# Per-head sums of squares in two float32r products, one quarter later, and the first values scaled ahead of a half subtraction

## The chip, the cores and the metric

The kernel runs on one core of one Trainium2 chip. The metric is device microseconds of one execution, inputs and output in the chip's memory; lower is better. A kernel's time is the median of its runs.

## The reference

Two transformer blocks on 256 tokens of width 1024, in float32. The change is in the second block's mixer, in the part that goes through heads. Cut to what matters:

```python
q_g = l2norm(cq.reshape(B, S, GDN_QK_HEADS, GDN_DK)) * GDN_DK ** -0.5
k_g = l2norm(ck.reshape(B, S, GDN_QK_HEADS, GDN_DK))
# l2norm(x) = x * rsqrt(sum(x * x over the 128 features of a head) + 1e-6)
kb = k * beta[..., None]
A = where(strict, einsum('bhntk,bhnsk->bhnts', kb, k) * Lmat, 0.0)
T = triangular_solve(eye + A, eye)                 # unit lower triangle, per chunk
u = matmul(T, v * beta[..., None]); w = matmul(T, kb * exp(gam)[..., None])
# per chunk: v_new = u - w S; o = (q exp(gam)) S + (q k^T Lmat) v_new; S = decayed S + k^T v_new
o_g = rmsnorm(o_g, gdn_out_norm) * silu(gz)        # and, beside it, the HGRN branch o_h
```

So for each head the squares of the convolved q and k are summed over the 128 features, which lie on the partitions: a product with a matrix of ones gives every partition the sum of each token's column.

## The kernel before, in words

**Exact products in pieces.** Weights arrive in chunks of 2048 columns x 128 partitions in a ring of three slots. ScalarE rounds a chunk to float32r (`split`, L590, or in halves with `split_part`, L597), VectorE writes the remainder (`low_of`, L1101; a whole chunk in `w_low`, halves in `w_low_half`), and TensorE does three float32r products for each one of the reference (`three`, L1860 to L1862; `three_x`, L1865 to L1867). A few small products inside a head use plain float32, and each of those shows as two MATMUL records.

**The heads.** One loop body `head(i, gemm, main)` runs on each of TensorE, ScalarE and VectorE, for i = 0 with `gemm` alone, for i = 1 to 7 in a hardware loop with both, and for i = 8 with `main` alone. The `gemm` part projects head i (six weight chunks), convolves, normalises and prepares its matrices; the `main` part does the recurrences of head i - 1: a level-by-level solve of the unit triangle (`inv_z`, L2365; `inv_w`, L2381; `inv_t`, L2390, with VectorE's masked merge `inverse`, L1638, and ScalarE's copies), the level-wise HGRN scores (L2342), the two chunks' values and the output. Order on each engine is the order of the written code; engines meet through semaphores only, and an engine that waits for one does nothing else.

**TensorE's order.** The projection is cut in 24 quarters of 12 products, 0 to 15 by column (256 columns each), 16 to 23 by token (512 columns each), and the small products stand between them by hand. Around the change, for i = 1 to 7: quarter 12; the first chunk's values (L2420, `vn0_done`); HGRN values (L2425 to L2427); quarter 13; wait for `vn0_ready`, the cross product L2440 (`cross_done`); quarter 14; wait for `r1_ready`, L2446 (`vn1_done`); wait for `sq_ready`, the sum of squares L2454 into bank 2 of M (`ss_done`); quarter 15; wait for `hsq_ready`, transposes of the gated HGRN output L2434 (`hss_done`); wait for `vn1_ready`, the output of the delta branch L2463 to L2465 (`go_done`); L2471 (`gam_done`); quarters 16 and 17; wait for `rs_ready`, L2480 (`vt_done`); quarter 18; L2242; quarter 19; L2492 and L2493 (`kq_done`); quarters 20 and 21; wait for `y0_ready`, the turned start of the solve L2502 (`t_done`); quarters 22 and 23. The next head begins with L2365, then again L2365 after VectorE's first merge (`xx_ready`).

**ScalarE's order** there: L997, L999, a table load, L1003, the squares L1004 (`sq_ready`); when `hpv_done` is there, `token_rstd` of the HGRN output (L930, L932, L934, `hrs_ready`); `split_j(2)` (L590, the chunk of quarters 20 to 23); when `ss_done` is there, the logarithm L1012 and exponential L1014 (`rs_ready`); when `hss_done` is there, L1022; when `go_done` is there, `token_rstd` of the delta output (L930, L932, L934, `grs_ready`); `split_j(3)`; L1031 (`v_ready`), L1033 (`lt_ready`), L1035 to L1039 (`lnf_ready`), L1041, L1049, `split_j(4)`, L1055 behind `y0_ready`, L1059 to L1065.

**VectorE's order** there: the last tap of the convolution (L1572, `conv_ready`); first half of a chunk's remainder (L1101; this chunk is for quarters 16 to 19); L1728, the first chunk's values times beta (`vn0_ready`); second half; L1736 (`r1_ready`); L1742; L1746 (`vn1_ready`); `hgrn_gate` (L1544, `hsq_ready`); `w_low_j(2)` (L1101, behind ScalarE's split 2); L1757 behind `rs_ready`; `delta_gate` (L1553, behind `grs_ready`); L1770 (`lt_pre`); L1772; a half chunk; L1776; L1779 behind `lnf_ready`; L1780; L1787; L1790; the drain L1791 (`y0_ready`); L1538; L1594; L1796; L1799 (`lt2_ready`); L1803; a half chunk; then the next head's `decayed` (L1608, L1609), a half chunk and the first `inverse` (L1638).

`settle()` is a drain of the engine's own pipeline. `xb` (hi and lo parts, 16 tiles of 256 columns each) takes the heads' results two tiles at a time; tiles 14 and 15 are those of the last head.

```python
def settle():
    v.drain()
def low_of(dst, src, hi):
    return v.tensor_tensor(dst, src, hi.bitcast(F32), ALU.subtract)
```

Of the kernel before, what the change touches and what calls it, by code (L numbers as in the profile page):

```python
# [6 lines left out]
ACT = mybir.ActivationFunctionType  # L7
AX_X = mybir.AxisListType.X
F32 = mybir.dt.float32
F32R = mybir.dt.float32r  # L10
# [3 lines left out]
P = 128  # L14
T = 256
# [14 lines left out]
RING = 3  # L30
# [53 lines left out]
def emit(nc, ctx, a, out):  # L84
    def sb(name, shape, dt=F32):
        return ctx.enter_context(nc.sbuf_tensor(name, shape, dt))

    def sem(name):
        return ctx.enter_context(nc.semaphore(name))
# [10 lines left out]
    res = sb("res", [P, TT, D])  # L100
    ident = sb("ident", [P, P])
    ones = sb("ones", [P, P])
    tri = sb("tri", [P, P])
    below = sb("below", [P, P])
    masks = sb("masks", [P, 2, 7, P])
# [89 lines left out]
    acc = grid(mix(4 * T), n=4, t=T)  # L195
# [61 lines left out]
    def yh_bank(tile):  # L257
# [50 lines left out]

    hpv_done, hsq_ready, hss_done, hrs_ready, hfin, lt2_ready, qk_ready = (
        sem(n) for n in ("hpv_done", "hsq_ready", "hss_done", "hrs_ready", "hfin", "lt2_ready", "qk_ready"))  # L310
    eh_ready, lnf_ready, dd_ready, lev_exp, wl_ready, lev_done, sc_used, tok_done, tok_ready = (
        sem(n) for n in ("eh_ready", "lnf_ready", "dd_ready", "lev_exp", "wl_ready", "lev_done", "sc_used", "tok_done",
                         "tok_ready"))

    conv_ready, tap_ready, sq_ready, ss_done, rs_ready, vt_done, v_ready, gbc_ready, gam_done, lt_pre, lt_ready = (
# [259 lines left out]
    def _(act):  # L575
# [263 lines left out]
        def head(i, gemm, main):  # L839
# [161 lines left out]
            if gemm:  # L1001
                settle()
                nc.scalar.activation(eh, G[:, 1, T:2 * T], ACT.Exp, scale=-1.0).then_inc(evac[1], 1)  # L1003
                nc.scalar.activation(eg[:, 0:2 * T], acc[:, 0:2, :].rearrange("p n t -> p (n t)"), ACT.Square).then_inc(sq_ready, 1)  # L1004
            if main:
                act.wait_ge(hpv_done, i)
                token_rstd(hrs.rearrange("p (i c) -> p i c", i=TT), M[:, 1, 0:T].rearrange("p (i c) -> p i c", i=TT),
# [86 lines left out]
    def _(dve):  # L1094
# [15 lines left out]
        def w_low_half(base, h, i=0, step=0):  # L1110
            slot = base % RING
            dve.wait_ge(hi_ready, base + i * step + 1)
            part = slice(CHUNK // 2 * h, CHUNK // 2 * (h + 1))
            ins = low_of(w_lo[:, slot, part], w_raw[:, slot, part], w_hi[:, slot, part])
            if h == 1:
                ins.then_inc(lo_ready, 1)
# [414 lines left out]
        v.memset(zd, 0.0)  # L1531
        settle()
        dve.wait_ge(built, BUILT_ALL)

        c0 = FIRST["heads"]

# [28 lines left out]
        def head(i, gemm, main):  # L1565
# [149 lines left out]
            if not main:  # L1715
# [4 lines left out]
                v.tensor_tensor(gams[:, :, 2, :], gams[:, :, 0, :], sums[:, 2], ALU.subtract)  # L1720
                settle()
                gam_copy()
            if gemm:
                w_low_half(c0 + 1 + RING, 0, i, 6)
            if main:
                dve.wait_ge(vn0_done, i)
                for e in range(2):
                    ins = v.tensor_scalar(vn0[:, e, :], M[:, 3, P * e:P * e + P], bst[:, 0, e:e + 1], None, ALU.mult)  # L1728
                ins.then_inc(vn0_ready, 1)
            if gemm:  # L1730
                w_low_half(c0 + 1 + RING, 1, i, 6)
            else:
                w_low_half(FIRST["yh"] + 2, 0)
            if main:
# [3 lines left out]
            if not gemm:  # L1738
                hgrn_gate(i)
            if gemm:  # L1740
                dve.wait_ge(evac[1], EV_HEADS[1] + 2 + i * 3)
                v.tensor_scalar(eh, eh, 2.0 ** 62, None, ALU.min).then_inc(eh_ready, 1)  # L1742
            if main:
                dve.wait_ge(vn1_done, i)
                for e in range(2):
                    ins = v.tensor_scalar(vn1[:, e, :], M[:, 3, T + P * e:T + P * e + P], bst[:, 1, e:e + 1], None, ALU.mult)  # L1746
                ins.then_inc(vn1_ready, 1)
                if not gemm:
                    dve.wait_ge(ohh_ready, 3)
                    gain_low(xa_lo[:, GH - 1, :], M[:, 1, T:2 * T], V_HN, xa_hi[:, GH - 1, :]).then_inc(ohl_ready, 1)  # L1750
                    w_low_half(FIRST["yh"] + 2, 1)
                else:
                    hgrn_gate(i)
            w_low_j(2)
            if gemm:
# [97 lines left out]
    def _(pe):  # L1853
# [425 lines left out]
        def head(i, gemm, main):  # L2279
# [150 lines left out]
            def hgrn_turned():  # L2430
                pe.wait_ge(hsq_ready, i)
                for b in range(TT):
                    blk = slice(P * b, P * b + P)
                    ins = nc.tensor.transpose(M[:, 1, T + P * b:T + P * b + P], hrs[:, blk], ident[:])  # L2434
                ins.then_inc(hss_done, 1)
# [13 lines left out]
                hgrn_turned()  # L2449
            if not main:  # L2450
                quarter(15)
            if gemm:
                pe.wait_ge(sq_ready, i + 1)
                mm(M[:, 2, :], ones[:], eg[:, 0:2 * T], start=True, stop=True).then_inc(ss_done, 1)  # L2454
            if main:
                quarter(15)
            if main and gemm:
                hgrn_turned()
            if main:
                pe.wait_ge(vn1_ready, i)  # L2460
                for e in range(2):
                    o = [M[:, 5, T * b + P * e:T * b + P * e + P] for b in range(TT)]
                    mm(o[0], lt[:, e, 0:P], vn0[:, e, :], start=True, stop=True)  # L2463
                    mm(o[1], lt[:, e, P:T], vn0[:, e, :], start=True, stop=False)
                    ins = mm(o[1], lt[:, e, T:3 * P], vn1[:, e, :], start=False, stop=True)  # L2465
                ins.then_inc(go_done, 1)
            if gemm:
                pe.wait_ge(gbc_ready, i + 1)
                for b in range(TT):
                    for e in range(2):  # L2470
                        ins = nc.tensor.transpose(M[:, 3, T * b + P * e:T * b + P * e + P],  # L2471
                                                  gst[:, b, e:e + 1].to_broadcast([P, P]), ident[:])
                ins.then_inc(gam_done, 1)
# [97 lines left out]
```

## Time and profile before

| | |
|---|---|
| runs, us | 1402.93, 1402.14, 1402.24; median 1402.24 |
| the profiled execution | 1402.24 us; span of its profile 1400.5 us |
| busy share | TensorE 99%, its weight loads 89%, VectorE 73%, ScalarE 57%, GpSimd 2% |
| granted TensorE clock | mean 0.999 of full speed |
| DMA | 224.90 MB, mean 161 GB/s |

The heads lie between about 700 and 1125 us of the span. Busy time counts an engine as busy while an instruction is in flight; TensorE's matmuls overlap each other, so a busy TensorE can still have gaps of a few tenths of a microsecond in its stream, which show as a wait of the weight load (PEld) or as a longer record. In a timeline, neighbours of one line are merged (x4 is four records), and in brackets stands the idle time before, with what ended it. "issue" names no engine.

### The profile page before, as it was taken

What the parts mean: (1) busy time and instruction counts of PE and PEld (TensorE: products, weight loads), DVE (VectorE), ACT (ScalarE), POOL (GpSimd) and SP (SyncE); (2) the same over time, 40 slices, a digit from 0 to 9 for tenths busy, and PEclk for the clock granted to TensorE, in tenths of its full rate; (3) what the DMA queues carried; (4) which work ended last, traced back from release to release, by engine and by line L of the source; (5) the groups of instructions that cost most, each with busy time, mean ns of one, the idle gap of its engine ahead of it and who ended that gap; (6) DMA issues with size and microseconds to landing.
All of it is one profiled execution on the core that took longest, in us unless ns stands there. A gap on an engine that the chain in (4) does not pass through costs nothing.

```text
span 1400.5 us, 25332 instructions
## 1 busy us (share of the span) xinstructions
PE 1381.5 (99%) x9112; PEld 1245.8 (89%) x9112; DVE 1028.9 (73%) x1597; ACT 801.4 (57%) x1307; POOL 28.1 (2%) x73
## 2 busy tenths in 40 slices
PE   8999999999999999999999999999999999999998
PEld 8999999988888878888899989989989898888887
DVE  5786776677666686666778888888888876666665
ACT  4445454544434454444668898898798843544443
POOL 6000000000000000000000000000000000000000
PEclk9999999999999999999999999999999999999999
DMA  8464454564555746665564444435434276566661
GB/s 271 139 181 143 129 148 150 179 215 154 202 186 182 231 129 184 200 186 180 151 181 121 121 119 123 131 105 141 127 94 147 72 199 211 159 182 196 199 195 60
DMA packets 296703, 224.90 MB, mean 161 GB/s; under 512 B 10675, under 2 KB 280133, under 8 KB 296645
## 3 DMA queue, kind: packets, MB, share of 16 engines
q1 hardware_dynamic: 296644, 224.09, 53.7%
q8 instruction: 40, 0.66, 0.2%
q14 instruction: 19, 0.15, 0.0%
HBM read 223.02 MB, written 1.05 MB: 160 GB/s over the span
## 4 chain that ended last, share of the span: by engine, by line
PE 87%; DVE 6%; DVEq 3%; ACT 2%; issue 2%; POOL 0%; ACTq 0%; POOLq 0%
PE M L1875 7%; PE G L1875 7%; PE G L1860 7%; PE G L1861 7%; PE G L1862 7%; PE M L1865 7%; PE M L1866 7%; PE M L1867 7%; PE G L1877 4%; PE M L1877 4%; DVEq L1098 2%; PE G L2526 2%; DVE arena L1572 2%; PE G L1865 1%; PE G L1867 1%
## 5 line engine op out<-in xcount | busy, mean ns | idle before, releaser
L1101 DVE TENSOR_TENSOR w_lo<-w_raw,w_hi 128x2048 fp32r<-128x2048 f32 (+2 forms) x249 | 480.7, 1935 | 172.2 <-ACT w_hi L590 169.9
L590 ACT ACTIVATE w_hi<-w_raw 128x2048 fp32r<-128x2048 f32 x198 | 377.4, 1908 | 179.5 <-PE G L1862 76.4
L1860 PE MATMUL G<-xa,w_hi 128*128 128x256 f32 x992 | 296.9, 299 | 0.0
L1862 PE MATMUL G<-xa,w_lo 128*128 128x256 f32 x992 | 280.4, 283 | 0.0
L1861 PE MATMUL G<-xa,w_hi 128*128 128x256 f32 x992 | 280.2, 282 | 0.0
L1860 PEld LDWEIGHTS G<-xa,w_hi 128*128 128x128 f32 x992 | 189.5, 191 | 3.5 <-issue 3.2
L1861 PEld LDWEIGHTS G<-xa,w_hi 128*128 128x128 f32 x992 | 189.6, 191 | 1.7 <-issue 1.7
L1862 PEld LDWEIGHTS G<-xa,w_lo 128*128 128x128 f32 x992 | 189.0, 191 | 0.0
L1865 PE MATMUL M<-w_hi,xb 128*128 128x512 f32 x304 | 118.8, 391 | 0.1
L1866 PE MATMUL M<-w_lo,xb 128*128 128x512 f32 x304 | 118.7, 390 | 0.0
L1867 PE MATMUL M<-w_hi,xb 128*128 128x512 f32 x304 | 118.3, 389 | 0.0
L1875 PE MATMUL M<-xa,w_hi 128*128 128x512 f32 x432 | 108.2, 392 | 0.0
L1875 PE MATMUL G<-xa,w_hi 128*128 128x512 f32 x432 | 107.3, 390 | 0.0
L784 ACT ACTIVATE arena<-arena 128x256 f32<-128x256 f32 x40 | 16.7, 419 | 143.5 <-DVE arena L1461 143.5
L1875 PEld LDWEIGHTS G<-xa,w_hi 128*128 128x128 f32 x432 | 79.7, 188 | 15.6
L1875 PEld LDWEIGHTS M<-xa,w_hi 128*128 128x128 f32 x432 | 77.7, 189 | 13.9
L1867 PEld LDWEIGHTS M<-w_hi,xb 128*128 128x128 f32 x304 | 57.1, 188 | 12.1
L1865 PEld LDWEIGHTS M<-w_hi,xb 128*128 128x128 f32 x304 | 57.2, 188 | 11.5 <-issue 0.5
L1866 PEld LDWEIGHTS M<-w_lo,xb 128*128 128x128 f32 x304 | 57.2, 188 | 10.5
L1877 PEld LDWEIGHTS M<-xa,w_lo 128*128 128x128 f32 x432 | 58.9, 190 | 4.2
L1877 PEld LDWEIGHTS G<-xa,w_lo 128*128 128x128 f32 x432 | 58.9, 190 | 4.2
L1877 PE MATMUL G<-xa,w_lo 128*128 128x256 f32 x432 | 60.2, 282 | 0.0
(385 smaller groups left out, 2531.9 us busy)
## 6 DMA issues: line engine op xcount, KB each, us to landing
w_raw<-in_w_in SPq DMA_DIRECT2D x150, 512.0 KB, 4.7
w_raw<-in_ffn_w_in SPq DMA_DIRECT2D x88, 512.0 KB, 5.0
w_raw<-in_w_ff SPq DMA_DIRECT2D x64, 512.0 KB, 4.2
w_raw<-in_ffn_w_out SPq DMA_DIRECT2D x44, 512.0 KB, 4.7
w_raw<-in_w_in SPq DMA_DIRECT2D x33, 256.0 KB, 3.2
w_raw<-in_w_out SPq DMA_DIRECT2D x16, 512.0 KB, 4.2
w_raw<-in_w_branch_gdn SPq DMA_DIRECT2D x16, 512.0 KB, 5.1
w_raw<-in_w_branch SPq DMA_DIRECT2D x12, 512.0 KB, 4.2
```

Source lines behind the costliest of these rows:

```text
L590: nc.scalar.activation(w_hi[:, slot, :], w_raw[:, slot, :], ACT.Copy).then_inc(hi_ready, 1)
L1098: v.drain()
L1101: return v.tensor_tensor(dst, src, hi.bitcast(F32), ALU.subtract)
L1572: ins = v.scalar_tensor_tensor(out=acc[:, n, :], in0=raw[:, n, 1 + j:1 + j + T], scalar=cwt[:, j, n:n + 1], in1=acc[:, n, :], op0=ALU.mult ...
L1860: mm(out_, w[0], x[0], start=first, stop=False)
L1861: mm(out_, w[0], x[1], start=False, stop=False)
L1862: return mm(out_, w[1], x[0], start=False, stop=last_)
L1865: mm(out_, x[0], w[0], start=first, stop=False)
L1866: mm(out_, x[0], w[1], start=False, stop=False)
L1867: return mm(out_, x[1], w[0], start=False, stop=last_)
L1875: mm(both_parts, wh[:, k, at:at + P], xa[:, :, k, :], start=k == 0, stop=False)
L1877: ins = mm(bank[:, 0:T], wl[:, k, at:at + P], xa_hi[:, k, :], start=False, stop=k == KT - 1)
```

## The change

The squares (256 columns of q, 256 of k) are rounded by ScalarE into tiles 14 and 15 of xb's high part; VectorE writes the remainder into those tiles of the low part and raises a new semaphore, `sql_ready`; TensorE adds a product of ones (now in float32r) with each of the two, in place of one float32 product. On TensorE this stands behind quarter 15 instead of in front of it (for i = 0 it stood behind it already), and the transposes of the gated HGRN output move behind the delta output's products. On VectorE the scaling of the first values moves in front of the first half subtraction; the first half comes behind it, the second half behind r1. hgrn_gate keeps its place, now behind the remainder.

```diff
@@ -100,6 +100,7 @@
     res = sb("res", [P, TT, D])
     ident = sb("ident", [P, P])
     ones = sb("ones", [P, P])
+    ones_r = sb("ones_r", [P, P], F32R)
     tri = sb("tri", [P, P])
     below = sb("below", [P, P])
     masks = sb("masks", [P, 2, 7, P])
@@ -1001,7 +1002,9 @@
             if gemm:
                 settle()
                 nc.scalar.activation(eh, G[:, 1, T:2 * T], ACT.Exp, scale=-1.0).then_inc(evac[1], 1)
-                nc.scalar.activation(eg[:, 0:2 * T], acc[:, 0:2, :].rearrange("p n t -> p (n t)"), ACT.Square).then_inc(sq_ready, 1)
+                nc.scalar.activation(eg[:, 0:2 * T], acc[:, 0:2, :].rearrange("p n t -> p (n t)"), ACT.Square)
+                settle()
+                nc.scalar.activation(xb_hi[:, 14:16, :].rearrange("p k t -> p (k t)"), eg[:, 0:2 * T], ACT.Copy).then_inc(sq_ready, 1)
             if main:
                 act.wait_ge(hpv_done, i)
                 token_rstd(hrs.rearrange("p (i c) -> p i c", i=TT), M[:, 1, 0:T].rearrange("p (i c) -> p i c", i=TT),
@@ -1531,6 +1534,8 @@
         v.memset(zd, 0.0)
         settle()
         dve.wait_ge(built, BUILT_ALL)
+        v.tensor_copy(ones_r[:], ones[:])
+        settle()
 
         c0 = FIRST["heads"]
 
@@ -1720,15 +1725,13 @@
                 v.tensor_tensor(gams[:, :, 2, :], gams[:, :, 0, :], sums[:, 2], ALU.subtract)
                 settle()
                 gam_copy()
-            if gemm:
-                w_low_half(c0 + 1 + RING, 0, i, 6)
             if main:
                 dve.wait_ge(vn0_done, i)
                 for e in range(2):
                     ins = v.tensor_scalar(vn0[:, e, :], M[:, 3, P * e:P * e + P], bst[:, 0, e:e + 1], None, ALU.mult)
                 ins.then_inc(vn0_ready, 1)
             if gemm:
-                w_low_half(c0 + 1 + RING, 1, i, 6)
+                w_low_half(c0 + 1 + RING, 0, i, 6)
             else:
                 w_low_half(FIRST["yh"] + 2, 0)
             if main:
@@ -1738,6 +1741,7 @@
             if not gemm:
                 hgrn_gate(i)
             if gemm:
+                w_low_half(c0 + 1 + RING, 1, i, 6)
                 dve.wait_ge(evac[1], EV_HEADS[1] + 2 + i * 3)
                 v.tensor_scalar(eh, eh, 2.0 ** 62, None, ALU.min).then_inc(eh_ready, 1)
             if main:
@@ -1749,7 +1753,11 @@
                     dve.wait_ge(ohh_ready, 3)
                     gain_low(xa_lo[:, GH - 1, :], M[:, 1, T:2 * T], V_HN, xa_hi[:, GH - 1, :]).then_inc(ohl_ready, 1)
                     w_low_half(FIRST["yh"] + 2, 1)
-                else:
+            if gemm:
+                dve.wait_ge(sq_ready, i + 1)
+                low_of(xb_lo[:, 14:16, :].rearrange("p k t -> p (k t)"), eg[:, 0:2 * T],
+                       xb_hi[:, 14:16, :].rearrange("p k t -> p (k t)")).then_inc(sql_ready, 1)
+                if main:
                     hgrn_gate(i)
             w_low_j(2)
             if gemm:
@@ -2449,13 +2457,13 @@
                 hgrn_turned()
             if not main:
                 quarter(15)
-            if gemm:
-                pe.wait_ge(sq_ready, i + 1)
-                mm(M[:, 2, :], ones[:], eg[:, 0:2 * T], start=True, stop=True).then_inc(ss_done, 1)
             if main:
                 quarter(15)
-            if main and gemm:
-                hgrn_turned()
+            if gemm:
+                pe.wait_ge(sql_ready, i + 1)
+                squares = [x[:, 14:16, :].rearrange("p k t -> p (k t)") for x in (xb_hi, xb_lo)]
+                mm(M[:, 2, :], ones_r[:], squares[0], start=True, stop=False)
+                mm(M[:, 2, :], ones_r[:], squares[1], start=False, stop=True).then_inc(ss_done, 1)
             if main:
                 pe.wait_ge(vn1_ready, i)
                 for e in range(2):
@@ -2464,6 +2472,8 @@
                     mm(o[1], lt[:, e, P:T], vn0[:, e, :], start=True, stop=False)
                     ins = mm(o[1], lt[:, e, T:3 * P], vn1[:, e, :], start=False, stop=True)
                 ins.then_inc(go_done, 1)
+            if main and gemm:
+                hgrn_turned()
             if gemm:
                 pe.wait_ge(gbc_ready, i + 1)
                 for b in range(TT):
```

The semaphore `sql_ready` is declared beside the others.

## Rows read from the trace of the kernel before

**Rows 1.** the page, first part: busy us, share of the span

```profile
PE 1381.5 (99%) x9112; PEld 1245.8 (89%) x9112; DVE 1028.9 (73%) x1597; ACT 801.4 (57%) x1307; POOL 28.1 (2%) x73
```

**Rows 2.** timeline (start, length, engine, line), TensorE, second solve product

```profile
741.96 0.62 PE L2365 MATMUL M<-arena 128*128 128x128 f32 x4
...
845.31 0.72 PE L2365 MATMUL M<-arena 128*128 128x128 f32 x4
...
896.90 0.72 PE L2365 MATMUL M<-arena 128*128 128x128 f32 x4
```

**Rows 3.** busy time by stretch, one turn of the head loop

```profile
core 0: us, PE busy (x) PEld busy (x) DVE busy (x) ACT busy (x) POOL busy (x), PEclk, DMA share, GB/s
...
840.80:892.40 51.60, 51.12 (x381) 47.84 (x380) 43.83 (x103) 43.76 (x102) 0.00 (x0) 1.00 0.45 122
```

**Rows 4.** timeline, VectorE, what that product waits for

```profile
896.11 0.73 DVE L1638 COPY_PREDICATED arena<-masks,M 128x256 f32<-128x256 int32 x1
```

**Rows 5.** waits of weight loads, 680 to 1060 us (total, times, longest)

```profile
PEld M L2440 <- DVE arena L1728: 3.9, 6, 0.7
```

**Rows 6.** timeline, VectorE, same turn, in order of time

```profile
870.22 1.23 DVE L1101 TENSOR_TENSOR w_lo<-w_raw,w_hi 128x1024 fp32r<-128x1024 f32 x1 [0.16 <-issue]
...
871.36 0.61 DVE L1728 TENSOR_SCALAR arena<-M,arena 128x128 f32<-128x128 f32 x2
...
874.64 0.61 DVE L1746 TENSOR_SCALAR arena<-M,arena 128x128 f32<-128x128 f32 x2 [1.01 <-PE M L2446]
...
876.79 2.29 DVE L1101 TENSOR_TENSOR w_lo<-w_raw,w_hi 128x2048 fp32r<-128x2048 f32 x1 [1.02 <-ACT w_hi L590]
...
880.31 1.13 DVE L1553 SCALAR_TENSOR_TENSOR arena<-M,arena 128x128 f32<-128x128 f32 x4 [0.22 <-ACT arena L934]
...
885.50 0.74 DVE L1779 TENSOR_TENSOR_SCAN arena<-ones,arena 128x128 f32<-128x128 f32 x2 [0.45 <-ACT arena L1039]
```

**Rows 7.** timeline, ScalarE, same turn

```profile
873.18 0.62 ACT L1004 ACTIVATE arena<-arena 128x512 f32<-128x512 f32 x1
...
873.70 0.27 ACT L930 ACTIVATE arena<-M 128x128 f32<-128x128 f32 x1
...
876.66 0.67 ACT L1012 ACTIVATE arena<-M,eps 128x512 f32<-128x512 f32 x1
...
877.40 0.63 ACT L1014 ACTIVATE arena<-arena 128x512 f32<-128x512 f32 x1
...
877.93 0.46 ACT L1022 ACTIVATE arena<-M,arena 128x256 f32 x1
...
878.49 0.28 ACT L930 ACTIVATE arena<-M 128x128 f32<-128x128 f32 x1
...
883.02 0.85 ACT L1033 ACTIVATE arena<-arena 128x768 f32<-128x768 f32 x1 [0.32 <-DVE arena L1770]
...
888.73 0.86 ACT L1055 ACTIVATE arena<-arena 64x256 f32<-64x256 f32 x2 [0.39 <-DVEq L1791]
```

**Rows 8.** timeline, TensorE, same turn: L2465 and L2502

```profile
878.07 0.39 PE L2465 MATMUL M<-arena 128*128 128x128 f32 x2
...
889.20 0.60 PE L2502 MATMUL M<-ident,arena 128*128 128x128 f32 x4
```

**Rows 9.** chain that ended last (start, length, what), same turn

```profile
874.60 0.86 PE M L2454 x2
...
879.12 0.23 PE G L1866
```

**Rows 10.** groups by line, 680 to 1060 us: nearest shapes

```profile
L1101 DVE TENSOR_TENSOR xa<-M,xa 128x512 fp32r<-128x512 f32 x4 | 2.6, 683 | 0.1
...
L771 ACT ACTIVATE arena<-res 128x512 f32<-128x512 f32 x1 | 0.6, 631 | 0.1
```

**Rows 11.** timeline, VectorE, first and last solve step

```profile
740.85 0.76 DVE L1638 COPY_PREDICATED arena<-masks,M 128x256 f32<-128x256 int32 x1 [0.72 <-PE M L2381]
...
1101.30 0.73 DVE L1638 COPY_PREDICATED arena<-masks,M 128x256 f32<-128x256 int32 x1 [0.25 <-PE M L2381]
```

More of the change, by code:

```diff
@@ L310, in emit @@
         sem(n) for n in ("hpv_done", "hsq_ready", "hss_done", "hrs_ready", "hfin", "lt2_ready", "qk_ready"))
-    eh_ready, lnf_ready, dd_ready, lev_exp, wl_ready, lev_done, sc_used, tok_done, tok_ready = (
-        sem(n) for n in ("eh_ready", "lnf_ready", "dd_ready", "lev_exp", "wl_ready", "lev_done", "sc_used", "tok_done",
+    eh_ready, sql_ready, lnf_ready, dd_ready, lev_exp, wl_ready, lev_done, sc_used, tok_done, tok_ready = (
+        sem(n) for n in ("eh_ready", "sql_ready", "lnf_ready", "dd_ready", "lev_exp", "wl_ready", "lev_done", "sc_used", "tok_done",
                          "tok_ready"))
```

## The prediction

> **What bounds the kernel now.** I read the page's busy times first: TensorE has something in flight for 99% of the span [rows 1]. That suggests that any TensorE work saved is time saved, and the next views test it. A turn of the head loop, from one occurrence of the second solve product (L2365) to the next, lasts 896.90 - 845.31 = 51.6 us [rows 2], and in it VectorE and ScalarE are each busy for about 43.8 us [rows 3], so both have about 8 us idle per turn. Where TensorE waits is what matters, and there are two places. The product L2365 has 0.72 us in the turns of 845.31 and 896.90 and 0.62 in the first, at 741.96 [rows 2]. It starts at 896.90, right behind the end of VectorE's merge L1638 at 896.11 + 0.73 = 896.84 [rows 4]: I estimate this stall at 0.2 us (0.1 of late start, 0.1 in the length). The other is L2440, whose weight load waits 3.9 us in 6 turns for L1728, so 0.65 each [rows 5]; L1728 stands behind a half subtraction of 1.23 us on VectorE [rows 6].
>
> Is the first of these stalls the end of a long chain, or an accident? I followed it backwards through the idle times. L1638 ends work that VectorE does without a wait of importance from L1779 at 885.50 on, apart from one at L1608 that names no engine. L1779 had waited 0.45 us for ScalarE's L1039 [rows 6], which follows L1033, which had waited 0.32 us for VectorE's L1770 [rows 7], which follows L1553, which had waited 0.22 us for ScalarE's L934 [rows 6]. That ends the reduction begun by L930 at 878.49 [rows 7], which started 0.03 us behind the end of TensorE's L2465, 878.07 + 0.39 = 878.46 [rows 8]. Each link has no slack. So the turn is set by a loop through three engines, TensorE to L2465, then ScalarE and VectorE in alternation to L1638, then TensorE again from L2365, and not by TensorE alone.
>
> **The change part by part.** *First values ahead of the half subtraction.* L1728 can start where the half subtraction starts now, 870.22, and its two parts end by 870.83. TensorE gets to L2440 about 0.6 us earlier. The half subtractions are late next, by 0.5 and 0.6 us (the second now also stands behind r1); their chunk is wanted only in quarter 16, behind L2465 and more than 4 us away, so this costs nothing.
>
> *The sum of squares.* One float32 product of 512 columns took 0.86 us of TensorE's time (the chain's view), and a float32r one of 512 columns 0.23 [rows 9]. Two of these make 0.46, so 0.40 is saved in each of eight heads. Should they run at 0.86 each, 0.86 is lost instead.
>
> *ScalarE's rounding copy.* 512 columns from SBUF took 0.63 us [rows 10]. The settle in front of it leaves 0.07 between L1012 (ends 877.33) and L1014 (877.40), and the next instruction starts 0.10 before the one ahead ends, as L1022 does at 877.93 behind L1014 (ends 878.03) [rows 7]. The square at 873.18 was followed by L930 at 873.70, 0.52 later [rows 7]; now it is 0.62 + 0.07 + 0.53 = 1.22. ScalarE's queue is therefore 0.70 us later from here on: the reduction of the HGRN output, split 2, the logarithm L1012, the exponential and L1022 all move. The bounds are 0.53, if the settle hides, and 0.77, if nothing overlaps. I take 0.70, since it is built from neighbours of the same width.
>
> *VectorE's remainder.* One subtraction of 512 columns, 0.68 us [rows 10]. It falls into time in which VectorE waits: 1.01 us in front of L1746 and 1.02 in front of w_low_j(2), for split 2 [rows 6]. Its own wait, for the copy, ends at 873.18 + 0.62 + 0.07 + 0.63 = 874.50. L1746, which follows a now earlier L2446, starts 0.6 sooner, at 874.04, and is done by about 874.65; the remainder, 0.1 overlapped, by 875.3. TensorE reaches the products at 874.60, where L2454 begins in the chain's view [rows 9], less 0.6 and plus quarter 15's twelve products of 0.12 (an estimate, half of the 0.23 of 512 columns), at 875.4. If this wait takes 0.1 us of TensorE, it is time that it loses again anyway (below). Behind it hgrn_gate waits for L934, 0.7 later, and w_low_j(2) for split 2, which ends 0.7 later: nothing is added to ScalarE's delay. Without that cover, the 0.68 would come on top in every turn.
>
> *The transposes moved behind go_done, and ones_r.* They cost the same and let L2465 come sooner; ScalarE gets to L1022 only at 878.6, more than a microsecond behind them. The copy of ones is 128 columns once, before the heads. No DMA is issued or moved; SyncE's and GpSimd's queues stay as they are.
>
> *The sum.* TensorE is 0.6 + 0.4 = 1.0 us earlier from quarter 16 on. But L930 for the delta output no longer waits for L2465: it now waits for ScalarE's queue. L1022 moves by 0.70, to 878.63, and L930 follows 0.35 behind it, at 878.98. Before, it had 878.49 - 877.93 - 0.35 = 0.21 of slack. The link of the loop moves by 0.70 - 0.21 = 0.49 us. All that follows moves with it: the first factors are ready at 888.73 + 0.49 = 889.22 (ScalarE's L1055 shows them at 888.73 [rows 7]), while TensorE would be there at 889.20 - 1.0 = 888.2 [rows 8]. It waits 1.0 us at L2502 and so gives all of its gain back. Then L1638 ends 0.49 later, and L2365 with it. A turn gets 0.49 us longer.
>
> Six turns give 6 x 0.49 = 2.94. In the first crossing, out of head 0, there is no delta output and no reduction on ScalarE, and VectorE's L1638 waited 0.72 us for TensorE [rows 11]: there TensorE sets the pace, and the cheaper product gains 0.40. In the last, L1638 had 0.25 us of wait left [rows 11], so only 0.49 - 0.25 = 0.24 arrives. In all 2.94 + 0.24 - 0.40 = 2.8 us. The profiled execution took 1402.24, of which 1400.5 is the span, and is itself the median of the three runs. So 1402.24 + 2.8 = 1405.0. With the copy's bounds (0.53 to 0.77, less slack 0.21, hence 0.32 to 0.56 a turn) the forecast's own range is 1403.8 to 1405.5.
>
> **Rivals.** *TensorE sets the pace (faster).* The stall at L2365 would be an accident of 0.2 us, and the chain behind it would give way once TensorE is earlier, for instance because the order of TensorE's work makes the other engines earlier too. For it: 99%, and a stall taken away that is seen in every turn. Against it: the idle times above, and that nothing in TensorE's order from quarter 16 on releases VectorE or ScalarE late. Its price is 7 x 1.0 + 0.4 = 7.4, so 1394.8. In a weaker form only the ready time at L2502 holds it back, at a distance of 889.20 - 888.73 = 0.47: 7 x 0.47 + 0.4 = 3.7, so 1398.5. It decides from the point where L2502 starts more than 0.1 us earlier in its turn than now. Chance 0.17 for both forms together.
>
> *The copy is absorbed.* ScalarE has more room between L1004 and L930 than the rows show. Then the gain is still given back at L2502, the turn stays 51.6 us, and only head 0 gains: 1401.8. Chance 0.15.
>
> *The delay is not shortened by the slack.* If the remainder ends later than the 875.3 above, or the settle costs more, the gate and w_low_j(2) start later, and the whole 0.70 arrives: 7 x 0.70 - 0.4 = 4.5, so 1406.7. Chance 0.06.
>
> *The change doesn't do what it says,* and the two products run at 0.86 each: TensorE is then at L2502 at 889.20 - 0.6 + 0.86 = 889.46 instead of waiting till 889.2, and at L2365 still before VectorE. The time is the forecast's, so it gets no chance of its own.
>
> *TensorE's clock.* It was granted 1.00 in this turn [rows 3], the level of 2.4 GHz, with stalls of 0.65 and 0.2 us in it. The forecast puts about 1.0 and 0.7 in their place. If the clock fell to 1.2 GHz for quarters 22 and 23 behind L2502, their twelve products of 0.23 [rows 9], 2.8 us, would take twice that: 7 x 2.8 = 20 us, so 1425. The Trainium skill, TensorE: Matmul & The Clock Gate, section "A second HAM failure mode: psum-queue depth-cycling", describes such a kernel, whose TensorE idles briefly and often and whose clock keeps changing level; this trace speaks against it. Chance 0.02.
>
> **How the numbers follow.** The forecast has 0.60. About 0.2%, 2.8 us, is what a measurement can tell from no change, and the forecast lies just on that bound: half of its chance goes to slower, half to same. Slower: 0.30 + 0.06 + 0.02 = 0.38. Same: 0.30 + 0.15 = 0.45. Faster: 0.17. The range goes from 1398.5, the faster rival's weaker form, to 1407, the delay without its slack, and leaves out that rival's full form and the clock.
>
> **What would show it.** In the changed profile: no wait of L2440's weight load; a new wait of about 1 us at L2502 for VectorE's drain; the stall in front of the second L2365 grown from 0.2 to 0.6 us or more; turns of 52.1 us; no idle between L1022 and L930. A turn of 51.1 us or less, or an L2502 without a wait, makes the prediction wrong.

## The result and the profile after

| | before | after |
|---|---|---|
| median of 19 runs each, us | 1402.26 (1402.14 to 1402.93) | 1404.74 (1404.47 to 1405.76) |
| profiled execution / span, us | 1402.24 / 1400.5 | 1405.76 / 1404.0 |

The change makes the kernel slower by 2.48 us: the ratio is 1.0018, with a 95% interval of 1.0011 to 1.0024. The prediction was 1405.0.

In the profile the code after the edited places has other line numbers: the second solve product is L2373 (before: L2365), the first chunk's cross product L2448 (L2440), the products of ones L2465 and L2466 (L2454), the delta output L2471 to L2473 (L2463 to L2465), the turned start L2512 (L2502); on ScalarE L931, L1025, L1036, L1058 (L930, L1022, L1033, L1055); on VectorE L1549, L1558, L1778, L1787, L1799, L1643 (L1544, L1553, L1770, L1779, L1791, L1638).

The page's first part, of the changed kernel, against [rows 1]. TensorE's busy time is 0.4 us less, VectorE's 6 us and ScalarE's 3.5 us more. (The cheaper products alone take 8 x 0.40 us out of TensorE's work, but a record that waits counts as busy, and the changed kernel has more of those.)

```profile
PE 1381.1 (98%) x9112; PEld 1244.8 (89%) x9112; DVE 1035.0 (74%) x1606; ACT 804.9 (57%) x1315; POOL 28.7 (2%) x73
```

The busy time by stretch, of one turn of the changed kernel (columns as in [rows 3]). The turn is half a microsecond longer, with the same number of TensorE records in it, and the granted clock is still 1.00, the level of 2.4 GHz:

```profile
840.80:892.90 52.10, 51.14 (x381) 47.77 (x380) 44.64 (x103) 44.25 (x104) 0.00 (x0) 1.00 0.45 121
```

The waits of TensorE's weight loads, 680 to 1060 us (total, times, longest), of the changed kernel, against [rows 5]:

```profile
PEld M L2512 <- DVEq L1799: 7.3, 6, 1.2
...
PEld M L2373 <- DVE arena L1643: 2.1, 6, 0.4
...
PEld M L2373 <- issue: 1.4, 6, 0.3
...
PEld M L2465 <- DVE xb L1104: 0.8, 5, 0.2
```

The wait at the cross product (L2440 before, 3.9 us in six turns) is gone. In its place TensorE waits 7.3 us in six turns for VectorE's drain at the turned start of the solve, 1.2 us each: the removed waiting has been given back at a later point, and a little more with it. The wait at the second solve product, where the weight load had waited 0.2 us in a single turn before, now shows in each. The row with "issue" is the first solve product, which has the same line: its weight load now waits 0.23 us. The row names no engine, but the load starts at 893.91, 0.12 behind the end of VectorE's L1807 (L1799 before), which raises the `lt2_ready` that this product waits for.

The timeline of ScalarE in the changed kernel, the turn of [rows 7] (start, length, engine, line; in brackets the idle time before):

```profile
874.57 0.63 ACT L1005 ACTIVATE arena<-arena 128x512 f32<-128x512 f32 x1
...
875.27 0.63 ACT L1007 ACTIVATE xb<-arena 128x512 fp32r<-128x512 f32 x1
...
875.80 0.26 ACT L931 ACTIVATE arena<-M 128x128 f32<-128x128 f32 x1
...
878.76 0.67 ACT L1015 ACTIVATE arena<-M,eps 128x512 f32<-128x512 f32 x1
...
880.03 0.46 ACT L1025 ACTIVATE arena<-M,arena 128x256 f32 x1
...
880.38 0.27 ACT L931 ACTIVATE arena<-M 128x128 f32<-128x128 f32 x1
...
884.97 0.85 ACT L1036 ACTIVATE arena<-arena 128x768 f32<-128x768 f32 x1 [0.45 <-DVE arena L1778]
```

The rounding copy (L1007, 0.63 us) starts 0.70 behind the square, and L931 follows 0.53 later. At 880.38 the reduction of the delta output starts 0.35 behind L1025, with no idle time before it. The last product of the delta output had ended on TensorE at 878.36 + 0.39 = 878.75 (the next view), so the reduction comes 1.63 us behind it, where [rows 7, 8] show 0.03. ScalarE no longer waits for TensorE there; it is late by its own queue.

The timeline of TensorE, same turn:

```profile
876.68 0.50 PE L2465 MATMUL M<-xb,ones_r 128*128 128x512 f32 x1
...
877.01 0.39 PE L2466 MATMUL M<-xb,ones_r 128*128 128x512 f32 x1
...
878.36 0.39 PE L2473 MATMUL M<-arena 128*128 128x128 f32 x2
...
890.68 0.66 PE L2512 MATMUL M<-ident,arena 128*128 128x128 f32 x4 [0.81 <-DVEq L1799]
...
898.40 0.28 PE L1870 MATMUL G<-xa,w_lo 128*128 128x256 f32 x1
...
898.83 0.72 PE L2373 MATMUL M<-arena 128*128 128x128 f32 x4 [0.15 <-DVE arena L1643]
```

The first product of ones takes 0.33 us to the start of the second (the wait for the remainder is in it), the second 0.23. L2512 has TensorE idle for 0.81 us in front of it. The second solve product starts 0.43 behind the product before it (898.40), which takes 0.12; before it followed after 0.21. It starts at 898.83, 52.07 us after its start at 846.76 in the turn before.

The timeline of VectorE, same turn, against [rows 6]:

```profile
875.32 0.61 DVE L1750 TENSOR_SCALAR arena<-M,arena 128x128 f32<-128x128 f32 x2
...
875.93 0.69 DVE L1104 TENSOR_TENSOR xb<-arena,xb 128x512 fp32r<-128x512 f32 x1
...
877.08 0.61 DVE L1549 SCALAR_TENSOR_TENSOR arena<-M,arena 128x128 f32<-128x128 f32 x2 [0.46 <-ACT arena L935]
...
878.88 2.29 DVE L1104 TENSOR_TENSOR w_lo<-w_raw,w_hi 128x2048 fp32r<-128x2048 f32 x1 [1.19 <-ACT w_hi L591]
...
882.02 0.17 DVE L1770 COPY arena<-arena 128x8 f32 x1
...
882.26 1.12 DVE L1558 SCALAR_TENSOR_TENSOR arena<-M,arena 128x128 f32<-128x128 f32 x4
...
898.04 0.73 DVE L1643 COPY_PREDICATED arena<-masks,M 128x256 f32<-128x256 int32 x1
```

The remainder (`xb`, 0.69 us) fits between the scaling of the second chunk's values (L1750) and the HGRN gate, which then still waits 0.46 us for ScalarE; the chunk's remainder waits 1.19 for split 2. One row is not as I had described it. The delta gate at 882.26 has lost the wait for ScalarE that it had at 880.31 [rows 6]: VectorE's own small copy in front of it ends at 882.02 + 0.17 = 882.19, while ScalarE's last L935, not shown, ended at 881.95 + 0.21 = 882.16. So VectorE's own way ends 0.03 us behind ScalarE's. With the drain it is 0.07: the gate starts 0.07 behind the end of VectorE's copy, with a drain between, and started 0.03 behind the end of ScalarE's L934 before (880.28 to 880.31).

The chain of work that ended last (start, length, what; "q" is an engine's sequencer), same turn. Between 872 and 890 it ran through TensorE before (two of its steps there are [rows 9]). Now it leaves TensorE at 864.73 and comes back at 898.83:

```profile
864.27 0.46 PE M L2368 x4
...
875.27 0.63 ACT xb L1007
...
876.95 1.91 ACT w_hi L591
...
878.88 2.29 DVE w_lo L1104
...
882.02 0.17 DVE arena L1770
...
882.26 0.41 DVE arena L1558 x2
...
884.97 0.85 ACT arena L1036
...
898.83 0.72 PE M L2373 x4
```

From TensorE's solve product it goes down ScalarE's queue to the rounding copy and split 2, then through VectorE's whole chunk, the normalisation and the small copy to the gate, and on as the prediction had it. TensorE's products in between, the delta output among them, are no link of it.

**Turns, from one second solve product to the next,** in us, read from TensorE's timeline as in [rows 2]. There are seven crossings, from the loop body of i = 1 to that of i = 2, and so on up to i = 8:

```
          1st    2nd    3rd    4th    5th    6th    last
before   51.76  51.59  51.59  51.59  51.57  51.57  50.46
after    51.99  52.06  52.07  52.06  52.04  52.05  50.64
longer    0.23   0.47   0.48   0.47   0.47   0.48   0.18
```

The seven differences sum to 2.78 us. In front of them, the second solve product of the body i = 1 starts at 742.71 instead of 741.96 [rows 2], 0.75 later. But the heads' first product (L2312 before, L2320 after) had started 1.15 us later, at 700.07 instead of 698.92; head 0 itself thus gained 0.40. Together, 2.78 + 0.75 is the 3.5 us between the two spans. The 1.15 us from before the heads belong mostly to this one execution, which took 1.0 us more than the median of the kernel's runs. Without them 2.78 - 0.40 = 2.38 remains, and the medians differ by 2.48.

### The profile page after: what moved, and what is told of

It reads as the page before. It is cut to its first block, busy times and chain, and to the rows that moved or that the text cites. A ratio compares the mean times of both kernels' runs of the same rounds, so it can differ in the third digit from the quotient of the medians.

```text
span 1404.0 us, 25358 instructions
## 1 busy us (share of the span) xinstructions
PE 1381.1 (98%) x9112; PEld 1244.8 (89%) x9112; DVE 1035.0 (74%) x1606; ACT 804.9 (57%) x1315; POOL 28.7 (2%) x73
## 4 chain that ended last, share of the span: by engine, by line
PE 76%; DVE 9%; ACT 8%; DVEq 3%; issue 2%; ACTq 1%; DMA 0%; SPq 0%
PE M L1883 7%; PE G L1883 7%; PE G L1868 7%; PE G L1870 7%; PE G L1869 7%; PE M L1873 6%; PE M L1874 6%; PE M L1875 6%; PE G L1885 4%; PE M L1885 4%; DVE w_lo L1104 3%; DVEq L1101 2%; PE G L2536 2%; ACT w_hi L591 2%; ACTq L578 1%
## 5 line engine op out<-in xcount | busy, mean ns | idle before, releaser
L1870 PE MATMUL G<-xa,w_lo 128*128 128x256 f32 x992 | 280.5, 283 | 0.0
L1104 DVE TENSOR_TENSOR xb<-arena,xb 128x256 fp32r<-128x256 f32 (+1 forms) x68 | 35.3, 519 | 34.2 <-ACT xb L787 21.3
```

What stands on the lines that cost most here:

```text
L1870: return mm(out_, w[1], x[0], start=False, stop=last_)
```

## The experiments

The theory is the prediction's: the turn is set by a loop through three engines, which the rounding copy on ScalarE lengthens. The rivals are that the price lies in VectorE's remainder or order, in TensorE's new products, or in the order of TensorE's work. Each kernel has its median from runs that alternate with the kernel before on the same chip; the ratio is to that. In these runs the kernel before had medians of 1402.61 to 1402.67, where it had 1402.26 beside the changed kernel, so two kernels are compared by the third column, in which the change itself has +2.48. "turn" is the length of the five middle crossings, which agree with one another within 0.05 us.

| kernel | us | against before | ratio (95%) | turn |
|---|---|---|---|---|
| e1, before + scaling first | 1401.29 | -1.38 | 0.9991 (0.9982 to 1.0000) | 51.46 |
| e2, before + ScalarE's copy | 1406.30 | +3.63 | 1.0026 (1.0016 to 1.0035) | 52.16 |
| e3, after, scaling back | 1405.20 | +2.53 | 1.0018 (1.0009 to 1.0027) | 52.08 |
| e4, after, copy twice | 1409.96 | +7.29 | 1.0051 (1.0038 to 1.0065) | 52.77 |
| e5, after, VectorE rounds | 1401.33 | -1.29 | 0.9991 (0.9982 to 1.0000) | 51.54 |
| e6, after, products twice | 1405.63 | +3.01 | 1.0022 (1.0013 to 1.0031) | 52.08 |
| e7, e5 + two moves | 1401.64 | -0.98 | 0.9993 (0.9984 to 1.0002) | 51.61 |
| e8, e5 + transposes back | 1400.33 | -2.28 | 0.9984 (0.9975 to 0.9993) | 51.40 |
| e9, e5 + reduction first | 1400.30 | -2.31 | 0.9983 (0.9974 to 0.9992) | 51.40 |
| e10, e9 + half chunks | 1398.27 | -4.34 | 0.9969 (0.9957 to 0.9981) | 51.06 |

### e1: the scaling ahead of the half subtraction, alone, on the kernel before

```diff
-                w_low_half(c0 + 1 + RING, 0, i, 6)
             if main:
                 dve.wait_ge(vn0_done, i)
...
             if gemm:
-                w_low_half(c0 + 1 + RING, 1, i, 6)
+                w_low_half(c0 + 1 + RING, 0, i, 6)
...
             if gemm:
+                w_low_half(c0 + 1 + RING, 1, i, 6)
                 dve.wait_ge(evac[1], EV_HEADS[1] + 2 + i * 3)
```

> The kernel before, with only the first values scaled ahead of the half subtractions. Theory (a loop through TensorE up to the delta output's product, then ScalarE and VectorE in alternation, then TensorE from the second solve product): TensorE gets to the delta output's product 0.6 us earlier, but ScalarE's queue has only 0.21 us of room in front of its reduction, so a turn goes from 51.6 to 51.4 us and the time to about 1401.0 us. Rival (TensorE's own order sets the pace): all of the 0.6 us arrives in 7 turns, about 1398 us.

Measured: 1401.29, turns of 51.46. The timelines of ScalarE and VectorE of e1:

```profile
877.90 0.46 ACT L1022 ACTIVATE arena<-M,arena 128x256 f32 x1
...
878.26 0.27 ACT L930 ACTIVATE arena<-M 128x128 f32<-128x128 f32 x1
...
879.89 0.17 DVE L1761 COPY arena<-arena 128x8 f32 x1
...
880.14 1.13 DVE L1553 SCALAR_TENSOR_TENSOR arena<-M,arena 128x128 f32<-128x128 f32 x4
```

L930 now starts right behind L1022, as expected, and the delta gate L1553 starts without a wait, behind VectorE's own copy. TensorE is 0.6 us earlier at the cross product, and of this 0.13 arrives in a middle turn (in the last crossing, 50.03 instead of 50.46, 0.43). The rest stops at queues: VectorE's own takes over before ScalarE's slack of 0.2 is used up, as its row 879.89 + 0.17, right in front of the gate, shows. So this half of the change is good by itself, for about a fifth of the waiting that it removes.

### e2: ScalarE's copy alone, on the kernel before

The copy's result is used by nobody; the float32 product of ones stays as it was.

```diff
                 nc.scalar.activation(eg[:, 0:2 * T], acc[:, 0:2, :].rearrange("p n t -> p (n t)"), ACT.Square).then_inc(sq_ready, 1)
+                settle()
+                nc.scalar.activation(xb_hi[:, 14:16, :].rearrange("p k t -> p (k t)"), eg[:, 0:2 * T], ACT.Copy)
```

> The kernel before, with only ScalarE's settle and rounding copy of 512 columns added behind the squares; nothing reads the copy, TensorE and VectorE keep their programs. Theory: ScalarE's queue is 0.70 us later, 0.21 of it is absorbed, a turn goes to 52.07 us and the time to about 1405.1 us, as in the changed kernel but without head 0's gain of 0.4. Rival (the cost of the change lies in the new wait for the remainder or in the moved products): 1402.3 us, unchanged.

Measured: 1406.30, turns of 52.16. With nothing of the change but this one ScalarE instruction and its drain, a turn gets 0.57 us longer, more than the whole change costs (0.48). VectorE's remainder and TensorE's products are absent here, so neither is the cause. The timeline of VectorE of e2, in the turn that starts at 847.11, shows where the 0.09 us beyond my 0.48 comes from:

```profile
882.44 0.17 DVE L1764 COPY arena<-arena 128x8 f32 x1
...
882.68 0.61 DVE L1555 SCALAR_TENSOR_TENSOR arena<-M,arena 128x128 f32<-128x128 f32 x2
```

ScalarE's last L934 ends 35.48 us behind the start of the turn, where it ended 34.97 behind it before: 0.51 later, so on this way about the forecast's slack was absorbed. But VectorE's own copy ends at 35.50 instead of 34.78, 0.72 later, and with the drain behind it comes last; this way had only 0.15 of slack (in the turn of [rows 6] the copy, not shown, ends at 880.09, with the drain at 880.16, and the gate starts at 880.31), so the gate is 0.57 later. In the changed kernel the gate is only 0.50 later, since ScalarE's L998 (L997 before and in e2) begins 24.72 us into the turn instead of 24.78, behind VectorE's last tap, which is 0.06 earlier too. Why the taps are earlier there I did not trace.

### e3: the whole change with the scaling's order undone

The edit is the reverse of e1's.

> The changed kernel, with the first values scaled between the two half subtractions again. Theory: the time stays at 1404.7 us; TensorE waits 0.6 us at the cross product again and about 0.6 us less at the turned start of the solve. Rival: the stall costs what it lasts, 7 x 0.6, about 1409 us.

Measured: 1405.20 and turns of 52.08, the same as the changed kernel (+2.53 against +2.48, 52.06). The waits of weight loads of e3 (seven turns):

```profile
PEld M L2449 <- DVE arena L1733: 4.6, 7, 0.7
...
PEld M L2513 <- DVEq L1800: 4.3, 7, 0.6
```

The wait at the cross product is back with its old 0.65 us, and the one at the turned start has shrunk by the same amount, from 1.2 to 0.6, with the turn unchanged. That is the plainest picture of this case: once the copy sets the turn, a stall of 0.65 us in every turn on an engine that is busy for 98% of the span costs nothing, since TensorE would wait at the next place anyway.

### e4 and e6: the copy doubled, the products doubled

e4 does `settle()` and the copy twice, e6 does the pair of ones products twice into the same bank.

> The changed kernel with ScalarE's settle and rounding copy done twice. Theory: no room is left in ScalarE's queue, so each turn gets 0.70 us longer, 52.8 us, and the time rises by 5 x 0.70 and something less in the first and last turn, to about 1409 us. Rival (ScalarE is off the path; the change's cost is VectorE's subtraction or the wait for it): the copies end 0.7 us later and TensorE's new wait grows out of time it loses anyway, 1404.7 to 1405.5 us.

> The changed kernel with the pair of products with ones done twice, 0.46 us more TensorE work in each of eight heads. Theory: in heads 1 to 7 it comes out of the 1.0 us that TensorE waits for the turned start of the solve, and only head 0 shows it: about 1405.2 us, turns of 52.07 us. Rival (TensorE sets the pace): 8 x 0.46 more, 1408.4 us.

Measured: e4 1409.96, turns of 52.77, longer by 0.71; e6 1405.63, turns of 52.08, longer by 0.02. The waits of e6:

```profile
PEld M L2514 <- DVEq L1799: 5.3, 7, 0.8
```

The second copy arrives in full, since neither way to the delta gate has slack left; each of the seven crossings is 0.71 or 0.72 longer, the first and the last too, where I had expected less: a copy with its drain costs 0.70 us of ScalarE's queue, as the prediction's sum had it. The 0.46 us of added TensorE work are taken out of the wait at the turned start (0.8 each instead of 1.2). Against the kernel before, e6 has +3.01 and the change +2.48. These 0.53 us lie mostly in head 0, where TensorE does set the pace: from the heads' first product to the first crossing it takes 43.14 us in e6 and 42.64 in the changed kernel. The seven crossings together add 0.14.

### e5: VectorE rounds instead of ScalarE

```diff
-                settle()
-                nc.scalar.activation(xb_hi[:, 14:16, :].rearrange("p k t -> p (k t)"), eg[:, 0:2 * T], ACT.Copy).then_inc(sq_ready, 1)
...
                 dve.wait_ge(sq_ready, i + 1)
+                v.tensor_copy(xb_hi[:, 14:16, :].rearrange("p k t -> p (k t)"), eg[:, 0:2 * T])
+                settle()
                 low_of(xb_lo[:, 14:16, :].rearrange("p k t -> p (k t)"), eg[:, 0:2 * T],
```

> The changed kernel with the rounding copy done by VectorE, directly in front of its remainder, instead of by ScalarE. Theory: VectorE does it in time in which it waits, ScalarE's queue is as before the change, and TensorE's earlier delta output lets ScalarE's reduction start 0.21 us earlier than before: turns of 51.4 us, head 0's 0.4 us kept, about 1400.6 us, faster than both kernels. Rival (the squares' new way to TensorE costs the time, whoever rounds): TensorE waits longer for the remainder, 1404.7 us or more.

Measured: 1401.33, turns of 51.54. The same rounding, one engine further on, turns +2.48 us into -1.29. The timelines of e5:

```profile
873.89 0.42 DVE L1756 CAST xb<-arena 128x512 fp32r<-128x512 f32 x1
...
874.38 0.69 DVE L1102 TENSOR_TENSOR xb<-arena,xb 128x512 fp32r<-128x512 f32 x1
...
876.21 2.29 DVE L1102 TENSOR_TENSOR w_lo<-w_raw,w_hi 128x2048 fp32r<-128x2048 f32 x1 [0.61 <-ACT w_hi L591]
...
879.74 1.13 DVE L1556 SCALAR_TENSOR_TENSOR arena<-M,arena 128x128 f32<-128x128 f32 x4 [0.23 <-ACT arena L935]
...
876.82 0.63 ACT L1015 ACTIVATE arena<-arena 128x512 f32<-128x512 f32 x1
...
877.56 0.47 ACT L1023 ACTIVATE arena<-M,arena 128x256 f32 x1
...
877.93 0.27 ACT L931 ACTIVATE arena<-M 128x128 f32<-128x128 f32 x1
```

VectorE takes 0.42 us for the copy that took ScalarE 0.63, and still waits 0.61 for split 2 behind it: it has the room that ScalarE has not. The turn is 0.1 longer than I expected. ScalarE's L1023 starts 0.74 behind L1015, where L1022 followed L1014 after 0.53 [rows 7]: the transposes that the change put behind the delta output are now what it waits for (TensorE ends them at 877.41). The prediction had costed that move at nothing, which holds in the changed kernel only because ScalarE is late there.

### e7: the delta reduction first on ScalarE, the gate first on VectorE

On top of e5, ScalarE does the copy of the turned HGRN output (L1022 before) behind the reduction of the delta output, and VectorE does the normalisation of q and k (L1757 before) and the memset and small copy behind it after L1770's.

```diff
+            if main:
+                act.wait_ge(go_done, i)
+                token_rstd(zi.rearrange("p i e c -> p (i e) c"), M[:, 5, :].rearrange("p (x c) -> p x c", c=P), o_sum, o_rstd,
+                           1.0).then_inc(grs_ready, 1)
             if gemm:
                 if main:
                     act.wait_ge(hss_done, i)
...
             w_low_j(2)
-            if gemm:
-                dve.wait_ge(rs_ready, i + 1)
-                v.tensor_tensor(acc[:, 0:2, :].rearrange("p n t -> p (n t)"), acc[:, 0:2, :].rearrange("p n t -> p (n t)"),
-                                eg[:, 2 * T:4 * T], ALU.mult).then_inc(qn_ready, 1)
...
             if main and gemm:
                 delta_gate(i)
```

> As the run in which VectorE rounds, and two more steps taken out of the loop: ScalarE copies the turned HGRN output behind the delta output's reduction instead of in front, and VectorE normalises q and k behind the decay differences instead of in front of the delta gate. Theory: ScalarE's reduction starts up to 0.35 us earlier still, VectorE follows, and its own work then becomes the bound after about 0.1 to 0.3 us of that: turns of 51.1 to 51.3 us, 1399 to 1400.3 us. Rival (the loop is no longer the bound once ScalarE's copy is gone): as the run in which VectorE rounds, 1400.6 us.

Measured: 1401.64, turns of 51.61, a miss: nothing gained. The timeline of VectorE of e7:

```profile
879.97 1.13 DVE L1556 SCALAR_TENSOR_TENSOR arena<-M,arena 128x128 f32<-128x128 f32 x4 [0.66 <-ACT arena L935]
...
881.01 1.64 DVE L1769 TENSOR_SCALAR arena<-M,arena 128x128 f32<-128x128 f32 x6
...
882.56 0.68 DVE L1772 TENSOR_TENSOR arena<-arena 128x512 f32<-128x512 f32 x1
```

The gate now waits 0.66 us for ScalarE, time in which VectorE could have done the normalisation. The gate starts 0.54 us earlier in its turn than in e5 (34.40 against 34.94), but the moved steps add 1.17 us behind L1769, and only some 0.5 of that falls into time in which VectorE waited for ScalarE in e5 (0.45 of idle time in front of the scan, L1787): the work in front of the drain ends 0.1 us later than in e5. I had moved work out of a gap into the loop.

### e8 and e9: two ways to take the transposes off ScalarE's path

e8 is e5 with TensorE's transposes in front of the delta output again, as before. e9 is e5 with e7's move on ScalarE alone; VectorE keeps its order.

> As the run in which VectorE rounds, with the HGRN output's transposes back in front of the delta output's products. In that run ScalarE's copy of the turned HGRN output began 0.1 us later than its queue allows, right behind the transposes' end. Theory (ScalarE's queue up to its second reduction is the loop): this wait goes, turns of 51.44 instead of 51.54 us, about 0.7 us less, 1400.6 us. Rival (the 0.1 us is absorbed, since VectorE is not ready earlier either): 51.54 us and 1401.3 us.

> As the run in which VectorE rounds, with ScalarE's copy of the turned HGRN output behind the delta output's reduction; VectorE's order is left alone. ScalarE's reduction ends 0.4 to 0.6 us earlier. Theory: VectorE's own queue (the remainder of split 2, the normalisation, the small copies) then reaches the delta gate last, 0.15 us earlier than in that run: turns of 51.4 us, about 1400.4 us. Rival (only ScalarE bounds the loop): 51.0 us, about 1398 us.

Measured: 1400.33 and 1400.30, turns of 51.40 for both, as expected. In the timelines of e8 and of e9, the first row is ScalarE's first reduction of the delta output, the second VectorE's gate:

```profile
877.52 0.27 ACT L931 ACTIVATE arena<-M 128x128 f32<-128x128 f32 x1
...
879.39 1.13 DVE L1556 SCALAR_TENSOR_TENSOR arena<-M,arena 128x128 f32<-128x128 f32 x4
```

```profile
877.15 0.26 ACT L931 ACTIVATE arena<-M 128x128 f32<-128x128 f32 x1
...
879.39 1.13 DVE L1556 SCALAR_TENSOR_TENSOR arena<-M,arena 128x128 f32<-128x128 f32 x4
```

In e9 ScalarE is 0.37 us earlier than in e8, and VectorE's gate starts at the same place in both, without a wait. So ScalarE's order is not the bound any more. What is in front of the gate on VectorE is the whole chunk of 2.29 us, which waits 0.64 for ScalarE's whole split 2 of 1.90.

### e10: split 2 and its remainder in halves

```diff
-            split_j(2)
+            if gemm:
+                split_part(c0 + 2 + RING, 0, i, 6, True)
+                split_part(c0 + 2 + RING, 1, i, 6)
...
-            w_low_j(2)
+            if gemm:
+                dve.wait_ge(sq_ready, 2 + i * 2)
+                slot = (c0 + 2 + RING) % RING
+                low_of(w_lo[:, slot, 0:CHUNK // 2], w_raw[:, slot, 0:CHUNK // 2], w_hi[:, slot, 0:CHUNK // 2])
+                w_low_half(c0 + 2 + RING, 1, i, 6)
```

(The fifth argument makes `split_part` raise `sq_ready` behind the first half; the wait for the squares becomes 1 + i * 2.)

> As the run before, with split 2 and its remainder in two halves, so that VectorE begins when ScalarE has done the first half. VectorE is at the delta gate 0.9 us earlier, at the price of 0.1 us on ScalarE for one more instruction. Theory: ScalarE's reduction is the bound again, 0.5 us earlier than in the run in which VectorE rounds: turns of 51.1 us, 1398.3 to 1398.9 us, the fastest of all. Rival (something else, TensorE's own work among it, holds the turn at 51.4 us): 1400.4 us.

Measured: 1398.27, turns of 51.06. The timeline of VectorE of e10:

```profile
874.78 2.35 DVE L1106 TENSOR_TENSOR w_lo<-w_raw,w_hi 128x1024 fp32r<-128x1024 f32 x2
...
878.53 1.13 DVE L1560 SCALAR_TENSOR_TENSOR arena<-M,arena 128x128 f32<-128x128 f32 x4 [0.38 <-ACT arena L937]
```

VectorE starts the chunk without a wait, behind the HGRN gate. At the delta gate it waits 0.38 for ScalarE again, so the bound has gone back to ScalarE, and the turn is 0.34 shorter than in e9. This is the fastest kernel of the study, 4.34 us below the kernel before, where the change as it was made is 2.48 above it, with the same products and squares as the change.

## Why the prediction was right

**The loop.** The forecast's case came true: not TensorE, 98% busy, but ScalarE and VectorE in alternation up to the first merge set the turn. The rows that it asked for are there: no wait at the cross product, a new one at the turned start (1.2 us; predicted 1.0), turns of 52.06 (52.1), and no idle time between L1025 and L931. The stall in front of the second solve product grew less than I had said: the start is 0.31 late instead of 0.09, so with the 0.1 in the record's length it went from 0.2 to 0.4, not to 0.6. TensorE itself comes later to it than I had said: by 0.03 at L2512 (0.02 forecast), by 0.08 more up to the first solve product, and by 0.15 more there, where it waits for VectorE (the row with "issue"); with the 0.22 at the second product this is the 0.48 of the turn. e2 and e4 show that the copy is the cause, e3 and e6 that TensorE's time is not.

One link was described incompletely. The prediction has ScalarE's reduction L931 release the gate 0.49 later. It does (882.16), but the delayed split 2 brings VectorE's own queue there just as late, by way of a chunk of 2.29 us, and it is this that comes last (by 0.03 us, or 0.07 with the drain behind it). The forecast's way had 0.21 us of slack, this one 0.15. That the gate moved by 0.50, where 0.49 was forecast, is in part luck: two omissions of 0.06 cancel, the smaller slack and the square that begins 0.06 earlier in its turn. Without the second, in e2, a turn grows by 0.57. For mending the change the second way matters: e9 moved only the reduction, e7 shortened both ways but put the work behind the gate, and only e10 shortened both without that.

**The terms.** The copy moved ScalarE's queue by 0.70 (875.27 - 874.57, with the square's 0.53 now behind the copy), and by 0.71 when doubled. The turn grew by 0.48 where 0.70 - 0.21 = 0.49 was forecast. The remainder took 0.69 (0.68), inside VectorE's wait, and cost TensorE 0.16 in a weight load wait (0.1), which it gave back later. The products took 0.23 each, apart from this wait; the rival in which they run at float32's rate is out. Head 0 gained 0.40 (0.40).

**The step that was mis-sized** is "Six turns give 6 x 0.49 = 2.94". The six crossings from the 1st to the 6th grew by 2.60: five of them by 2.37 together, the 1st by only 0.23. (The prediction's "first crossing, out of head 0" lies in front of these; it is the 0.40 of head 0.) The kernel before has a wait of its own in the 1st crossing, and in no other; the timeline of VectorE before:

```profile
757.58 0.88 DVE L1572 SCALAR_TENSOR_TENSOR arena<-arena 128x256 f32<-128x256 f32 x2 [0.21 <-issue]
```

Up to this tap of the convolution VectorE is 0.12 us earlier in its turn than in the third crossing, and from it on 0.13 later, which stays so to the gate. The changed kernel has no idle time there and is 0.10 earlier all the way. So 0.25 us that the kernel before loses in this turn is not lost in the changed one. What the tap waits for is not shown. The last crossing was longer by 0.18 instead of 0.24. The sum of measured terms is 2.60 + 0.18 - 0.40 = 2.38, against the forecast's 2.8, and the medians say 2.48.

**The rivals.** "TensorE sets the pace" fell with L2512's wait; e1 shows what was true in it, 0.13 us a turn. "The copy is absorbed" fell with e2. "The delay is not shortened by the slack" fell with the 0.48; the slack was real, and e4, with no slack left, pays 0.71. The clock stayed at 1.00 in the turn shown, in which weight loads wait 1.2 us at L2512 and 0.35 and 0.23 us at L2373, so a pause of that size between products did not cost it here; the Trainium skill's case of a kernel whose clock keeps changing level (TensorE: Matmul & The Clock Gate, "A second HAM failure mode: psum-queue depth-cycling") is not this one.

**What it had not seen.** The prediction priced the move of the transposes at nothing, which is right for this change only. With the copy gone from ScalarE they cost 0.14 us a turn (e5 against e8).

## What to carry to other kernels

A busy share near 100% does not name the pacer. Follow the short waits backwards from the first stall until the walk comes back to its start: if every link starts at once when it is released, as here, that loop sets the turn, and work off it costs nothing until its slack is used up. Look for the second-latest way into each link too, since a gain ends at it. Where an added operation can go to either of two engines, give it to the one that waits right before the result is wanted (here VectorE: -1.29 us against +2.48), not to the one on which the loop's next link is queued. When two engines hand a long tile to each other, a hand-over in halves can shorten the loop more than a reordering (here 0.34 us a turn in e10, against 0.14 in e8 and e9).

## What was not expected of the hardware

VectorE's copy of 512 float32 columns into float32r took 0.42 us (e5, L1756) where ScalarE's took 0.63 and VectorE's subtraction of the same width 0.69: on VectorE a rounding copy costs no more than a plain copy of this width within SBUF (L1780 in e5, 0.42).
